# The last two tiles of the input loop in a two-layer decoder trunk: heads turned first, gated product ahead of the taps, twelve taps in attention

## What is computed

```
a = RMSNorm(h);  z = a @ w_in            # split: 512 for SGU, 512 for conv, 416 for attention
y_a = SGU(z_sgu)                         # gelu, layer norm, a 128x128 mix over tokens
y_b = conv(a_half * sigmoid(g_half))     # 31 taps per channel, 256 channels, then norm, silu, matrix
q, k, v from z_mla                       # 8 heads, q and k of 96 values, normalised, rotary
y_c = causal softmax attention(q, k, v)
h += [norm(y_a) | norm(y_b) | norm(y_c)] @ w_o
h += expert layer;  h += gated embedding
```

## Time and profile before

| | |
|---|---|
| median of 3 runs | 2148.43 us (2143.27 to 2148.58) |
| profiled execution | 2146.81 us, span 2145.0 us |
| busy share of the span | PE 93%, PEld 52%, DVE 48%, ACT 30%, POOL 17% |
| chain that ended last | PE 76%, DMA 12%, DVE 5%, issue 3% |

### The profile page before, as it was taken

One profiled execution on the slowest core, in us unless ns is written; L12 is line 12 of the kernel. 1 busy time (PEld: TensorE's weight loads), 2 busy tenths in 40 slices (PEclk: granted clock), 3 DMA queues, 4 the chain that ended last, 5 costly groups with the idle time before them and its releaser, 6 DMA issues.

```text
span 2145.0 us, 35269 instructions
## 1 busy us (share of the span) xinstructions
PE 1985.8 (93%) x8952; PEld 1109.6 (52%) x8952; DVE 1030.5 (48%) x2327; ACT 640.1 (30%) x1521; POOL 374.1 (17%) x542
## 2 busy tenths in 40 slices
PE   6999799999869999999979997999998699999898
PEld 3555466655535455544435554666555354455443
DVE  3489768754341111135434897787543411111353
ACT  3333366622111111131133432666221111111311
POOL 2232100021012222210022321000210122222100
PEclk9999999999979999999989997999999799999999
DMA  7011251000489999965310111510004899999522
GB/s 255 15 29 29 53 164 31 26 20 30 162 326 391 380 383 376 388 228 206 89 29 15 29 29 47 170 32 25 20 30 167 309 391 380 382 373 368 181 92 98
DMA packets 122224, 362.00 MB, mean 169 GB/s; under 512 B 18853, under 2 KB 54005, under 8 KB 105220
## 3 DMA queue, kind: packets, MB, share of 16 engines
q1 hardware_dynamic: 105028, 318.74, 41.1%
q0 software_dynamic: 14784, 33.59, 4.2%
q10 hardware_dynamic: 2304, 8.39, 1.0%
HBM read 319.50 MB, written 59.51 MB: 177 GB/s over the span
## 4 chain that ended last, share of the span: by engine, by line
PE 76%; DMA 12%; DVE 5%; issue 3%; ACT 1%; SPq 1%; DVEq 0%; POOL 0%; ACTq 0%; POOLq 0%
PE ps L1829 31%; DMA region_c<-in_moe_w_up_dram 8%; PE ps L2202 7%; PE ps L1992 6%; PE ps L1850 4%; PE ps L2198 4%; PE ps L2035 4%; PE ps L2223 3%; PE ps L1798 3%; PE ps L2014 3%; PE ps L2217 2%; PE ps L1924 2%; DMA region_a<-in_moe_w_up_dram 2%; PE ps L2183 2%; PE ps L2124 2%
## 5 line engine op out<-in xcount | busy, mean ns | idle before, releaser
L1829 PE MATMUL ps<-region_b,region_c 128*128 128x512 f32 x1024 | 447.9, 593 | 2.7 <-DVE region_c L1291 2.7
L1829 PEld LDWEIGHTS ps<-region_b,region_c 128*128 128x128 f32 x1024 | 191.7, 190 | 226.5 <-issue 226.0
L1829 PE MATMUL ps<-region_a,region_c 128*128 128x512 f32 x512 | 225.4, 594 | 0.0
L1709 DVE SCALAR_TENSOR_TENSOR region_a<-region_a,ps 128x128 f32<-128x128 f32 x66 | 23.4, 354 | 386.0 <-ACT region_a L1154 386.0
L2202 PE MATMUL ps<-region_c,region_a 128*128 128x512 f32 x336 | 148.8, 596 | 13.3 <-DMA region_c<-in_moe_w_up_dram 13.3
L1992 PE MATMUL ps<-region_c 96*128 96x512 f32 (+3 forms) x384 | 155.6, 515 | 5.6 <-DMA region_c<-qk_heads 2.8
L1829 PEld LDWEIGHTS ps<-region_a,region_c 128*128 128x128 f32 x512 | 96.9, 191 | 117.8 <-issue 117.8
L1154 ACT ACTIVATE region_a<-ps 128x128 f32<-128x128 f32 x66 | 21.8, 331 | 363.6 <-PE ps L2202 243.1
L2202 PEld LDWEIGHTS ps<-region_c,region_a 128*128 128x128 f32 x336 | 62.1, 190 | 93.4 <-issue 93.4
L1486 DVE TENSOR_REDUCE neg_max<-ps 128x1 f32<-128x128 f32 (+7 forms) x128 | 96.7, 756 | 24.2 <-PE ps L1999 21.1
L954 ACT COPY region_c<-ps 128x512 f32<-128x512 f32 x48 | 28.1, 585 | 244.9 <-PE ps L1798 174.2
(11 more groups left out here) (360 smaller groups left out, 3187.5 us busy)
## 6 DMA issues: line engine op xcount, KB each, us to landing
region_c<-in_moe_w_gate_dram SPq DMA_DIRECT2D x44, 1024.0 KB, 10.4
region_c<-in_moe_w_up_dram SPq DMA_DIRECT2D x44, 1024.0 KB, 17.2
region_c<-in_moe_w_down_dram SPq DMA_DIRECT2D x44, 1024.0 KB, 12.9
region_a<-in_moe_w_gate_dram SPq DMA_DIRECT2D x22, 1024.0 KB
region_a<-in_moe_w_up_dram SPq DMA_DIRECT2D x22, 1024.0 KB
region_a<-in_moe_w_down_dram SPq DMA_DIRECT2D x22, 1024.0 KB, 12.9
region_c<-choice_outputs SPq DMA_DIRECT2D x32, 512.0 KB, 4.4
qk_heads<-gains SPq DMA_DIRECT2D x32, 384.0 KB, 4.0
```

The source lines that it names most:

```text
L1829: ins = mm(dst, lhsT[:, k, :], w[:, k, a:b], start=(k == 0), stop=(k == KD - 1))
```

## The change

1. **PE, ACT: heads first.** After step 7 the order on PE becomes q(6), k(6), q(7), mix(7), k(7), turn of the gated product (7). On ACT the copies of q(7) and k(7) come ahead of the copies of tile 7's gated product (`z_cin`).
2. **DVE: gated product ahead of the taps.** `gelu_glu` of tile t moves from the start of step t+1 to step t, behind the gate's scaling and ahead of the last 12 taps.
3. **DVE: twelve taps moved.** Taps 19 to 30 and the join of tile 4 leave step 7; attention carries them. Its steps with j = 2 and 3 now carry two taps where they carried one (14 a head, 105 in all, where it was 12 and 93).
4. **PE: waits split.** Of the ten semaphores ahead of attention six stay. ZT, ZG and ZC are waited for ahead of the scores of j = 5 of head 0, ZS ahead of the fifth transpose of step 4.

```diff
+    LATE_TAP = 19
...
 (ACT)
                 lag_loop(act, [(1, turn(0)), (-1, z_glu_tanh), (-2, turned("q", 0)), (3, norm(0)), (0, q_cnT), (1, z_mla), (-2, turned("k", 1)),
-                               (1, c_square), (0, prepare, 1), (0, q_evac), (-1, z_cin), (0, k_evac), (0, z_square), (0, z_tanh)])
+                               (1, c_square), (0, prepare, 1), (0, q_evac), (-1, z_cin), (0, k_evac), (0, z_square), (0, z_tanh)], after=False)
+                z_glu_tanh(TILES - 1, 1, PAIRS - 1)
+                for t in (TILES - 2, TILES - 1):
+                    turned("q", 0)(t, t % 2, PAIRS - 1)
+                    turned("k", 1)(t, t % 2, PAIRS - 1)
+                z_cin(TILES - 1, 1, PAIRS - 1)
...
 (DVE)
+                def conv_last(t, u, i):
+                    if u == 0:
+                        guarded(v, i < PAIRS - 2, lambda: conv(LATE_TAP, TAPS)(t, u, i))
+                    else:
+                        conv(LATE_TAP, TAPS)(t, u, i)
...
-                lag_loop(v, [(-1, gelu_glu), (2, norm(0)), (-3, conv(0, 8)), (-1, sgu_out), (1, c_norm), (0, q_sums), (-3, conv(8, 19)),
-                             (0, gelu_cubic), (0, gelu_gated), (0, gate_centre), (0, q_scale), (0, gate_scale), (-3, conv(19, TAPS))])
+                lag_loop(v, [(2, norm(0)), (-3, conv(0, 8)), (-1, sgu_out), (1, c_norm), (0, q_sums), (-3, conv(8, LATE_TAP)),
+                             (0, gelu_cubic), (0, gelu_gated), (0, gate_centre), (0, q_scale), (0, gate_scale), (0, gelu_glu), (-3, conv_last)])
...
+                CT_vec.resume(f"tap{LATE_TAP}")
...
-                    first = 12 * hd + j + max(j - 4, 0)
-                    for k in range(first, min(first + 1 + (j >= 4), 3 * TAPS)):
-                        taps(TILES - 3 + k // TAPS, (1 + k // TAPS) % 2, [k % TAPS], acc_last)
+                    first = 14 * hd + j + max(j - 2, 0) + LATE_TAP
+                    for k in range(first, min(first + 1 + (j >= 2), 4 * TAPS)):
+                        taps(TILES - 4 + k // TAPS, k // TAPS % 2, [k % TAPS], acc_last if k >= TAPS else acc_two)
...
 (PE)
                 lag_loop(pe, [(-2, r_turn("q", qs)), (1, z_mla), (0, q_cT), (-2, r_turn("k", ks)), (0, q_mm), (-1, mix_tokens), (-1, glu_turn),
-                              (0, kv_mm), (0, z_first), (2, turn(0)), (0, z_glu), (0, prepare, 0)])
+                              (0, kv_mm), (0, z_first), (2, turn(0)), (0, z_glu), (0, prepare, 0)], after=False)
+                r_turn("q", qs)(TILES - 2, 0, PAIRS - 1)
+                r_turn("k", ks)(TILES - 2, 0, PAIRS - 1)
+                r_turn("q", qs)(TILES - 1, 1, PAIRS - 1)
+                mix_tokens(TILES - 1, 1, PAIRS - 1)
+                r_turn("k", ks)(TILES - 1, 1, PAIRS - 1)
+                glu_turn(TILES - 1, 1, PAIRS - 1)
 
                 end = TILES * l + TILES
-                for s in (Z_act, ZM_act, ZT_act, Z_vec, ZG_vec, ZS_vec, ZC_act, QT_act, QM_act, KM_act):
+                for s in (Z_act, ZM_act, Z_vec, QT_act, QM_act, KM_act):
                     pe.wait_ge(*s.before(end))
                 settle(pe, passed)
...
+                    if head == 0 and j == 5:
+
+                        for s in (ZT_act, ZG_vec, ZC_act):
+                            pe.wait_ge(*s.before(end))
+                        settle(pe, passed)
...
                     for k in range(j + 1):
+                        if n == 4 and k == 4:
+                            pe.wait_ge(*ZS_vec.before(end))
```

More of the change, by code:

```diff
@@ L61, in next, with resume @@
         return self.sem, 1
+    def resume(self, name):
+        self.at = self.names.index(name)
     def after(self, index, name=None):
```

## The result

The changed kernel took **2131.58 us** (median of 4 runs, 2127.36 to 2135.56), the kernel before 2147.93 us beside it (4 runs, 2143.27 to 2148.58): a ratio of 0.9926, interval 0.9915 to 0.9938. 2132 us was forecast. The profiled execution took 2132.33 us, its span 2130.5 us.

The account below looks back on a forecast made before the run. PE was taken to bound the kernel, waiting for the gated product and then on a chain through the staging buffer. Gains of 6.2 and 8.9 us less 0.4 for taps, 14.7 us off 2146.81, gave 2132 us; range 2126 to 2140.

Parts of the forecast that it names:

- Step 7: End of the input loop: with the gated product early, q(6) starts 3.26 us earlier in layer 0, 6.19 in layer 1.
- the clock term of layer 1: From kv product to q(6) in layer 1: without PE's idling its clock stays up, gaining 0 to 2.72 us; 2.72 taken.
- The tail: From q(6) to k(7): heads first ends k(7) at 256.6 and 1327.7 us; gain including step 7 6.2 and 8.9 us.
- the wait behind q(7): Tail: the copy of q(7) waits 2 us for the staging buffer that the store of tile 6 still reads.
- Only step 7 pays: Rival for the tail: tile 6's store takes so long that the tail gives nothing; 2138 us, chance 0.10.
- No wait for the buffer: Rival for the tail: buffer free before q(7) is turned, DVE's heads set the time; 2126 us, chance 0.05.
- The estimate of 2.9 us for the store: Staging buffer's store in the tail: skill's fixed cost plus 384 KB gives 2.9 us; sum would reach some 20 us.
- From k(7) to the late scores: Copy, store and load between k(7) and the scores needing the last columns: same work, 10.5 us, unchanged.
- The waits: Four waits moved into attention: each costs nothing, covered by scores of j = 0 to 4; uncovered, ZC about 1 us.
- The taps: Twelve taps and a join per layer in attention's j = 2 and 3: 0.4 us lost over both layers, bounds 0 to 9.6.
- Taps on the path: Rival in attention: all 24 taps late by 0.40 us, 5.5 us of gain left; 2141 us, chance 0.10.
- Slower: Rival in attention: late maxima stall PE, clock falls, 2.72 us a head; 2176 us, decides from 6 heads, chance 0.04.

Follow-up runs that it names:

- e1_product: Kernel before with only the gated product moved ahead of the last 12 taps; 2134.79 us, ratio 0.994.
- e2_heads: Kernel before with only the new order of heads on PE and ACT and the split waits, taps and product as before; 2141.95 us, ratio 0.9978.
- e6_own_buffer: Changed kernel with a second staging buffer for tile 7 alone; 2132.23 us, ratio 0.9935 to the kernel before.
- e7_both: Changed kernel with 23 taps of tile 4 in attention in place of 12 and an own staging buffer for tile 7; 2121.20 us, ratio 0.989 to before.
- c1_before: Kernel before, unchanged, profiled a second time; 2144.23 us, one run.
- c2_before: Kernel before, unchanged, profiled a third time; 2148.02 us, one run.
- e4_waits: Changed kernel with all ten waits ahead of attention again; 2140.66 us, ratio 0.9968 to the kernel before.
- e9_one_wait: Changed kernel with only the wait for ACT's last copies of the gated product (ZC) put back ahead of attention; 2139.19 us, ratio 0.9971 to before.
- e3_taps: Changed kernel with the twelve taps and the join of tile 4 back in step 7, behind the gated product; 2132.15 us, ratio 0.993 to before.
- e5_more_taps: Changed kernel with 23 taps of tile 4 a layer moved into attention in place of 12; 2128.82 us, ratio 0.9916 to before.

## Why the prediction was right, and where it was not

**Step 7.** 3.26 and 6.19 us were forecast, 3.26 and 6.20 us came between the first two profiles; the clock term of layer 1, taken at 2.72 us between 0 and 2.72, came as taken. For layer 0 the row of one execution was taken as the kernel's. Over three profiles of before, A averages 21.66 and 22.27 us, so the product's place is worth 5.1 and 5.8 us, 10.9 together and not 9.4. e1_product, 13.4 us less by the medians, points the same way.

**The tail.** The end of k(7) was forecast at 256.6 us and came at 256.57 us. The reason holds: the store of tile 6 sets it. Copy to copy it held the buffer 5.25 us (5.14 was taken), in e2_heads 5.23 us. The size of the wait behind q(7) was off: 0.8 us, not 2 us, since q(7) itself ran from 250.80 to 252.72 us at the half clock. DVE had the heads at 250.23 us, as forecast (250.24), but the sum had q(7) start some 0.4 us sooner and run at the full clock, ending at 251.4 us, although it let PE idle 3 us ahead of it. That cost nothing, because the buffer came free later still. Of layer 1's 8.9 us for step 7 and tail, 6.20 + 2.55 = 8.75 us came.

*Only step 7 pays* fell with B at 12.6 us. *No wait for the buffer* fell as a forecast. e6_own_buffer is that case made true, and it moved the end of k(7) by 1.3 and 1.1 us and not by the 3 us a layer that the rival gave, which had q(7) and k(7) at the full clock; it takes the early heads as well, in e7_both, to get more. The estimate of 2.9 us for the store did not hold: on the chains of these profiles the later of a tile's two stores landed 4.35 to 4.47 us after its issue in 29 of 30 places and at 5.25 us in the other. The Trainium skill, DMA: Bandwidth & Descriptors, Anatomy of one DMA, fits its figure on transfers that GpSimd issues; SP issues these.

**From k(7) to the late scores** 10.5 us were taken as unchanged. In the changed kernel it was 9.31 and 9.05 us. This is the term that failed; c1_before and c2_before put it down for the most part to the one profile read, not to the change: they have 9.0 to 9.9 us with the old tail, the two profiles of the changed kernel 9.0 to 9.9 us as well.

**The waits.** "Each costs nothing, covered" held: PE's timeline has no such wait. "Uncovered, ZC would cost about 1 us" was too low: against the changed kernel's two profiles (9.0 to 9.9 us) stage C of e4_waits and e9_one_wait is 2.3 to 4.5 us longer a layer, the wait of 2 us and the half clock behind it. So the split is no ornament: with the new order of the heads and without the split more is lost there than the tail's 5.3 us.

**The taps.** DVE's timeline of layer 1, head 3, which answers to the earlier trace rows: the gaps of 0.45 and 0.37 us ahead of the masks are 0.20 and 0 us.

```profile
1384.33 0.30 DVE L1499 TENSOR_TENSOR ps<-ps,mask_b 128x128 f32<-128x128 f32 x1 [0.20 <-PE ps L2019]
...
1386.38 0.30 DVE L1499 TENSOR_TENSOR ps<-ps,mask_b 128x128 f32<-128x128 f32 x1
```

DVE is busy with 114.74 us of the window from 271 to 415 us where it was 110.00. 0.4 us of loss was taken; none can be seen in D, neither with 12 taps (the changed kernel against e3_taps) nor with 23 (e5_more_taps). *Taps on the path* and *Slower* fell; by its own price *Slower* would show only from 8 heads on (21.8 us against 14.7 + 6.4), not from 6. One sign that was named came otherwise: PE's waits for exponentials rose from 2.6 us (6 of them) to 4.0 us (8). Two of them, 0.8 us, are new in the first scores of layer 0, ahead of the load's landing, and cost nothing. The rest is later in attention, where one wait a layer grew from 0.44 to 0.7 us. PE's timeline of layer 0 in the changed kernel, then in e3_taps:

```profile
366.42 0.46 PE L2019 MATMUL ps<-region_c 96*128 96x128 f32 x2 [0.72 <-ACT region_a L1095]
```
```profile
366.90 0.46 PE L2018 MATMUL ps<-region_c 96*128 96x128 f32 x2 [0.44 <-ACT region_a L1095]
```

Both profiles of the changed kernel have the longer wait, and e3_taps, with the twelve taps back in step 7, has not: they cost PE 0.3 us a layer at this place, 0.6 us in all. D does not show even that: 150.4 to 150.5 us with them, 150.56 us in e3_taps.

**The sum** came out at 14.7 us against 14.5 us of span partly by errors that cancel, and that is luck. So is the 0.4 us between forecast and median: the medians differ by 16.4 us, and the sum was taken off a profiled execution 1.1 us under the median. With three profiles of before and two of the changed kernel the stages give 10.9 us (A), 5.3 us (B), 1.2 us (C) and 0.7 us (D), less 0.6 us in M and 2.6 us in E, and 0.2 us from the start of the kernel: 14.7 us. C and D rest in the main on the first profile of before: without it they are 0.6 and 0.1 us. E is the one open item: 650.5 and 649.9 us in the two profiles of the changed kernel, 647.3 to 648.2 in those of before. PE's longest waits on a transfer, for the gathered tokens of the experts, were 19.2 us in both layers together in the changed kernel's first profile and 17.5 us before. E holds only layer 1's, 9.6 us against 8.7 us, so 0.9 of the 3.2 us by which E differs there:

```profile
PE ps L2212 <- DMA region_a<-moe_inputs,block_tokens: 19.2, 2, 9.6
```

e3_taps, with the same order in the tail, has 17.1 us there and an E of 647.6 us, and e7_both, furthest ahead of all, has an E of 648.1 us. So an earlier attention does not bring the loss by itself; what does is not shown.

## What to carry to other kernels

Where an engine waits at two places one behind the other, price the removal of both: e5_more_taps and e6_own_buffer each moved B by at most 1.3 us, together by 4.9 us, of which 1.7 us are the clock. A wait that is moved onto PE's path costs its own length and the half clock behind it, here once more as much in the worst layer. And profile the kernel before more than once: a clock that fell in one layer and not in the other was a warning that the row is one of two outcomes.

## What the hardware showed that was not expected

The same wait of 3.05 us ahead of the gated product's turn left the clock alone in two of the eight places that have it (layer 0 of the first profile and of e2_heads, A at 19.8 us) and cost 1.5 to 3.0 us in the other six (A at 21.3 to 22.8 us). The Trainium skill, TensorE: Matmul & The Clock Gate, What's actually happening, says that the number of slow matmuls at a kernel's start varies from run to run of one kernel. The traces agree in the times: the first 16 products of the attention part (L1850, L1866 in the changed kernel) take 6.55 to 7.38 us in the five profiles of the two kernels and the next 16 take 5.82 or 5.83 us, though the windows show a granted clock of 1.00 there. Behind the wait of 3.05 us it varies besides whether the clock falls at all.

The way back differs as much. After a wait of 4.35 us the clock of e2_heads fell and was still at half in attention, 9 us behind the start of k(7) (257.86 us); after 4.38 us that of e5_more_taps was back some 3 us behind it (255.83 us). Windows of e2_heads, then of e5_more_taps:

```profile
257.00:262.00 5.00, 4.14 (x17) 3.48 (x18) 1.30 (x5) 2.40 (x6) 0.00 (x0) 0.50 0.00 0
262.00:268.00 6.00, 6.00 (x17) 2.87 (x18) 2.69 (x7) 2.65 (x8) 0.00 (x0) 0.56 0.65 167
```
```profile
257.00:262.00 5.00, 4.81 (x20) 3.09 (x18) 2.06 (x6) 3.20 (x10) 0.00 (x0) 0.79 0.34 83
262.00:268.00 6.00, 5.62 (x27) 3.42 (x27) 5.25 (x11) 4.22 (x10) 0.00 (x0) 1.00 0.68 185
```

It shows in stage C of layer 0: 10.7 us and 8.9 us. Why the one came back sooner is not shown.
